# Summing the squares of a LayerNorm's variance ahead of TensorE, with one product in place of five

## The chip, the cores and the metric

The kernel runs on one core of one Trainium2 chip. The metric is the time of one execution on the device, in microseconds (us). Five engines work side by side, each on its own list of instructions and joined only by semaphores: TensorE (PE in the profile), VectorE (DVE), ScalarE (ACT), GpSimd (POOL) and SyncE (SP, which here only issues DMAs).

## The reference

One inference step of a decoder of two layers, for 512 prompt tokens and 8 sequences of 8 sample tokens, all fp32, with D = 1024 features. Cut to what matters here, a layer is

```python
def _layer_norm(x, g, b):
    mu = jnp.mean(xf, axis=-1, keepdims=True)
    var = jnp.mean(jnp.square(xf - mu), axis=-1, keepdims=True)
    return ((xf - mu) * lax.rsqrt(var + LN_EPS) * g + b)

x = _layer_norm(ALPHA * x + 0.5 * _swiglu(x, ffn1...), ln1_g, ln1_b)
h = x @ w_in          # pooling, sliding-window attention, cross-attention, gates
x = _layer_norm(ALPHA * x + merged @ w_o, ln2_g, ln2_b)
x = _layer_norm(ALPHA * x + 0.5 * _swiglu(x, ffn2...), ln3_g, ln3_b)
```

So there are three LayerNorms in each layer and six in the kernel.

## The kernel before

**Layout.** The features lie on the 128 partitions in 8 chunks (`KC`), the 576 tokens along the free axis, in two halves of 288 (`TH`). `x[:, c, half(h)]` is a tile of 128 x 288. Every weight product is split into a rounded part and a rest of the weight and of the activation, so that a step of a product is three matmuls (`mm3`); it is called a triple below.

**A LayerNorm** is done for one token half after the other: n = 0, 1, 2 is the norm of the layer, h = 0, 1 the half. A half goes round the engines in this order:

- `mean(l, n, h)`: TensorE multiplies a matrix whose entries are all 1/1024 (`ones`) with sums of the chunks and so gets the mean of every token on all partitions, in the PSUM bank `TP`. For h = 0 and for n = 1 VectorE has kept a sum of chunks (`lnsum`) and one or two products do. For h = 1 of n = 0 and n = 2 there are five products: of the sums of chunks 0+1, 2+3 and 4+5, which GpSimd adds (`add_chunks`, L1743), and of chunks 6 and 7.
- `center` (L1415): VectorE subtracts the mean, eight instructions.
- `square` (L936): ScalarE squares each centered chunk into `squares(c)`.
- `add_squares` (L1738): GpSimd adds squares 0+1, 2+3 and 4+5 (`SQUARE_SUMS`).
- `variance` (L1976, L1979): TensorE multiplies `ones` with these three sums and with squares 6 and 7, five products, into the PSUM bank `S`. An fp32 product of `ones` is two instructions in the trace.
- `root` (L940): ScalarE takes the square root; `reciprocal` (L1420): VectorE.
- `scale` (L1426) on VectorE, then ScalarE rounds the scaled chunk (`xth`, `xh`), and VectorE or GpSimd makes its rest (`rest_of_x`: L1484, L1437; GpSimd: L1754). A chunk's rounded part and rest are what TensorE needs to begin the next products with that chunk.

**Order on TensorE.** It is written out by hand, and the products of `ones` are put between the triples of whatever weight product runs then:

- n = 0 and n = 2, h = 0: mean and variance lie in `tail` of the FFN before (`tail` runs h = 0 and then h = 1, each with 8 products of 4 triples; the variance stands in the third product of h = 1). A tail's results are added onto x by VectorE, two chunks at a time (`tail_onto_x`, L1402); the four of h = 1 are placed by hand between the steps of the norm of h = 0, and the mean of h = 1 needs all four.
- n = 0, h = 1: both lie in `project_first`, which multiplies the normed x by the first columns of `w_in`: first four chunks of one block, then two blocks in turn, then two blocks into the banks S and TP, and the same again for h = 1. The mean stands after the first three chunks, the variance ahead of the two last triples of the two blocks.
- n = 1: mean and variance of h = 0 lie in the products of `w_o` (outputs m = 4 and m = 5 of h = 1), those of h = 1 in `head` of the second FFN.
- n = 2, h = 1: in layer 0 both lie in `head` of the next layer's first FFN. In layer 1 nothing comes behind: the mean and eight products of `ones` (L2330) end the kernel, and the change leaves those eight alone.

**Order on the other engines.** VectorE's list for a half is `center`, then work of the FFN or of `w_o` that is ready by then, then `reciprocal`, `scale` and the rests. That work is `tail_onto_x` (n = 0 and 2), `residual` (n = 1: the products of `w_o` onto x and into `lnsum`, L1475 and L1478), or the rest of a weight block (`rest_w`, L1164, n = 0, h = 1). GpSimd's list mixes `add_squares`, `add_chunks` and the rests of the next head's weights (L1782), in a fixed order too; in `head` of GpSimd the sums of squares stand in front of the rest of one quarter of the weights.

Of the kernel before, what the change touches and what calls it, by code (L numbers as in the profile page):

```python
# [33 lines left out]
SQUARE_SUMS = (0, 2, 4)  # L34
# [142 lines left out]
def build(nc, wblk, wg, wd, wt_d, x0, mem0, cst_d, par_d, mks_d, mvs_d, kcs_d, vcs_d, sps_d,  # L177
          y_out, kT_out, v_out, poolp_out, pools_out, mk_out, mv_out, kc_out, vc_out):
    with ExitStack() as ctx:
# [175 lines left out]
        sq_ready, sq_sum, sq_used, std_ready, normed = sem("sq_ready"), sem("sq_sum"), sem("sq_used"), sem("std_ready"), sem("normed")  # L355
# [128 lines left out]
        def square_sum_count(l, n, h, c):  # L484
            return (l * 6 + 2 * n + h) * len(SQUARE_SUMS) + SQUARE_SUMS.index(c) + 1

# [10 lines left out]
        def chunk_sum_count(fb, w):  # L497
            return fb * 3 + w + 1
# [660 lines left out]
        def _(dve):  # L1159
# [256 lines left out]

            def reciprocal(l, n, h):

                dve.wait_ge(std_ready, l * 6 + 2 * n + h + 1)
                nc.vector.reciprocal(S[:, h, 0:TH], S[:, h, 0:TH])  # L1420
                dve.drain()
# [7 lines left out]
            def norm_plain(l):  # L1429

                fb = 2 * l

                def rest_of_x(h, c):
                    if c in BY_DVE:
                        b = par[:, P_LN + 8 + c:P_LN + 9 + c]
                        dve.wait_ge(x_hi, x_hi_count(l, h, c))
                        nc.vector.scalar_tensor_tensor(out=xl[:, c, half(h)], in0=x[:, c, half(h)], scalar=b,  # L1437
                                                       in1=xh[:, c, half(h)].bitcast(F32), op0=ALU.add,
                                                       op1=ALU.subtract).then_inc(x_lo, 1)

                center(l, 0, 0)
                tail_onto_x(fb, 0, 1)
                reciprocal(l, 0, 0)
                for c in range(KC):
                    scale(0, 0, c)
                    if c > 0:
                        rest_of_x(0, c - 1)
                    if c in (1, 3, 5):
                        tail_onto_x(fb, (c + 1) // 2, 1)
                rest_of_x(0, KC - 1)  # L1450
                rest_w(pq(l, Q_IN + 1), 0)
                center(l, 0, 1)
                dve.drain().then_inc(t_free, 1)
                rest_w(pq(l, Q_IN + 1), 1)
                reciprocal(l, 0, 1)
                for c in range(KC):
                    scale(0, 1, c)
                    if c == KC - 1:
                        dve.drain().then_inc(s_free, 1)
                    if c > 0:  # L1460
                        rest_of_x(1, c - 1)
                rest_of_x(1, KC - 1)

            def norm_head(l, n):
# [32 lines left out]
                else:  # L1497
# [3 lines left out]
                for c in range(KC):  # L1501
# [5 lines left out]
                    if n == 2 and c in (1, 4):  # L1507
                        tail_onto_x(fb - 1, 1 + c // 4, 1)
                rest_of_x(0, KC - 1)
                if n == 2:  # L1510
                    tail_onto_x(fb - 1, 3, 1)
                else:
                    residual(6, 1)
                    residual(7, 1)
                center(l, n, 1)
                dve.drain().then_inc(t_free, 1)
                reciprocal(l, n, 1)
# [10 lines left out]
            def norm_last(l):  # L1528
                center(l, 2, 0)
                tail_onto_x(2 * l + 1, 0, 1)  # L1530
                reciprocal(l, 2, 0)
# [200 lines left out]
        def _(pool):  # L1732

            def add_squares(l, n, h):

                for c in SQUARE_SUMS:
                    pool.wait_ge(sq_ready, norm_count(l, n, h, c + 1))
                    nc.gpsimd.tensor_tensor(squares(c), squares(c), squares(c + 1), ALU.add).then_inc(sq_sum, 1)  # L1738

            def add_chunks(fb, w):  # L1740
# [3 lines left out]
                                        ALU.add).then_inc(chunk_sum, 1)  # L1744

# [115 lines left out]
        def _(pe):  # L1861
# [34 lines left out]
            def project_first(l, qq, u):  # L1896
# [3 lines left out]
                for h in range(2):  # L1900
                    turns = [(c, 0) for c in range(lag)] + [(c - lag * s, s) for c in range(lag, KC) for s in range(2)]
                    for c, s in turns + [(c, 1) for c in range(KC - lag, KC)]:
# [11 lines left out]
                        if (h, c, s) == (0, 6, 1):  # L1914
                            variance(l, 0, 1)
                    for s, bank in enumerate((S, TP)):
# [7 lines left out]
                        for c in range(KC):  # L1924
                            last = mm3(lambda h: bank[:, h, 0:TH], wt(s, c), (xs(xh, c), xs(xl, c)), c, KC, (h,))
                        if h == 1:
# [21 lines left out]
            def mean(l, n, h):  # L1948
# [6 lines left out]
                if n != 1 and h == 1:  # L1955

                    fb = 2 * l + n // 2
                    for w in range(3):
                        pe.wait_ge(chunk_sum, chunk_sum_count(fb, w))
                        nc.tensor.matmul(TP[:, 1, 0:TH], ones, chunk_sum_place(w), start=w == 0, stop=False)  # L1960
                    pe.wait_ge(tail_add, tail_count(fb, 3, 1))
                    for c in (KC - 2, KC - 1):
                        last = nc.tensor.matmul(TP[:, 1, 0:TH], ones, x[:, c, half(1)], start=False, stop=c == KC - 1)
                    last.then_inc(mean_done, 1)
# [6 lines left out]
            def variance(l, n, h):  # L1971
                if h == 0:
                    pe.wait_ge(s_free, s_count(l, f"var{n}") + 1)
                for c in SQUARE_SUMS:
                    pe.wait_ge(sq_sum, square_sum_count(l, n, h, c))
                    nc.tensor.matmul(S[:, h, 0:TH], ones, squares(c), start=(c == 0), stop=False)  # L1976
                for c in (KC - 2, KC - 1):
                    pe.wait_ge(sq_ready, norm_count(l, n, h, c))
                    last = nc.tensor.matmul(S[:, h, 0:TH], ones, squares(c), start=False, stop=(c == KC - 1))  # L1979
                last.then_inc(sq_used, 1)  # L1980
# [46 lines left out]
            def head(fb):  # L2027
# [26 lines left out]
                def block(g, w, h):  # L2054
                    begin_block(g, w, h)
                    for c in range(KC):
                        chunk(g, w, h, c)
                        if fb and (g, w, h, c) == ((1, 0, 0, 1) if n == 1 else (1, 0, 0, 7)):
                            variance(l, n, 1)

                for h in range(2):

                    lag = (4, 2)[h]
                    for c in range(KC + lag):
# [9 lines left out]
                        if fb and (h, c) == (0, 4 if n == 1 else KC + 1):  # L2074
# [7 lines left out]
            def tail(fb):  # L2082
# [3 lines left out]
                for h in range(2):  # L2086
                    for p in range(KC):
# [7 lines left out]
                        for i in range(4):  # L2095
# [9 lines left out]
                            if (h, p, i) == (1, 2, 1):  # L2105
# [18 lines left out]
            for l in range(L):  # L2124
# [183 lines left out]
                for h in range(2):  # L2308
                    for m in WO_HALVES[h]:
# [8 lines left out]
                        for c in range(KC):  # L2318
# [3 lines left out]
                            if (h, m, c) == (1, 5, 5):  # L2322
# [165 lines left out]
```

## Time and profile before

| | |
|---|---|
| median of 3 runs | 2364.52 us (2363.46 to 2365.7) |
| profiled execution, its own time | 2364.38 us |
| its span, first to last instruction | 2362.6 us |
| mean granted TensorE clock | 0.998 of full speed |
| busy: TensorE / VectorE / ScalarE / GpSimd | 99% / 69% / 52% / 27% |

The span is what the trace covers; 1.8 us of the execution's own time lie around it. Times in the rows below are microseconds from the span's start, unless marked ns. The engine named behind `<-` in square brackets is the one that ended an idle time.

### The profile page before, as it was taken

What the parts mean: (1) busy time and instruction counts of PE and PEld (TensorE: products, weight loads), DVE (VectorE), ACT (ScalarE), POOL (GpSimd) and SP (SyncE); (2) the same over time, 40 slices, a digit from 0 to 9 for tenths busy, and PEclk for the clock granted to TensorE, in tenths of its full rate; (3) what the DMA queues carried; (4) which work ended last, traced back from release to release, by engine and by line L of the source; (5) the groups of instructions that cost most, each with busy time, mean ns of one, the idle gap of its engine ahead of it and who ended that gap; (6) DMA issues with size and microseconds to landing.
All of it is one profiled execution on the core that took longest, in us unless ns stands there. A gap on an engine that the chain in (4) does not pass through costs nothing.

```text
span 2362.6 us, 44967 instructions
## 1 busy us (share of the span) xinstructions
PE 2329.5 (99%) x17537; PEld 2281.7 (97%) x17537; DVE 1628.8 (69%) x2722; ACT 1218.0 (52%) x2478; POOL 646.5 (27%) x573
## 2 busy tenths in 40 slices
PE   8999999999999999999999999999999999999998
PEld 8999999999999999999999999999999999999997
DVE  4878786755445787878578787766544458877775
ACT  5655555455323565555565556554552236665654
POOL 1334334230000233333423333342200021333333
PEclk9999999999999999999999999999999999999999
DMA  6222224222222122232213322333122231222221
GB/s 239 93 104 87 94 94 158 69 91 60 72 82 97 72 81 99 90 108 90 90 54 110 108 90 87 111 128 107 56 66 76 86 116 49 89 97 92 98 99 58
DMA packets 54482, 221.29 MB, mean 94 GB/s; under 512 B 15904, under 2 KB 18848, under 8 KB 41184
## 3 DMA queue, kind: packets, MB, share of 16 engines
q1 hardware_dynamic: 54272, 218.41, 27.0%
q8 instruction: 141, 2.31, 0.4%
q14 instruction: 69, 0.57, 0.1%
HBM read 213.58 MB, written 6.04 MB: 93 GB/s over the span
## 4 chain that ended last, share of the span: by engine, by line
PE 89%; DVE 7%; ACT 2%; DVEq 1%; issue 1%; DMA 0%; POOL 0%; ACTq 0%; SPq 0%; POOLq 0%
PE pair L2022 14%; PE pair L2024 14%; PE pair L2023 14%; PE pair L1865 10%; PE pair L1869 10%; PE pair L1867 10%; PE S L2022 2%; PE S L2024 2%; PE S L2023 2%; PE TP L1869 1%; PE TP L1867 1%; PE TP L1865 1%; PE TP L2203 1%; DVE htl L1260 1%; PE TP L2182 1%; PE S L1976 1%
## 5 line engine op out<-in xcount | busy, mean ns | idle before, releaser
L2023 PE MATMUL pair<-xtl,hiA 128*128 128x288 f32 x1216 | 358.8, 295 | 0.0
L2024 PE MATMUL pair<-xth,loA 128*128 128x288 f32 x1216 | 358.4, 295 | 0.0
L2022 PE MATMUL pair<-xth,hiA 128*128 128x288 f32 x1216 | 358.3, 295 | 0.0
L1766 POOL TENSOR_TENSOR loB<-rawB,hiB 128x512 fp32r<-128x512 f32 (+1 forms) x128 | 174.6, 1365 | 448.9 <-ACT hiB L719 448.9
L719 ACT ACTIVATE hiA<-TP 128x512 fp32r<-128x512 f32 (+1 forms) x372 | 194.0, 556 | 150.0 <-DVE TP L1183 72.2
L1169 DVE TENSOR_TENSOR loA<-TP,hiA 128x512 fp32r<-128x512 f32 (+1 forms) x372 | 236.3, 635 | 16.4 <-ACT hiA L719 13.2
L1766 POOL TENSOR_TENSOR loB<-rawA,hiB 128x512 fp32r<-128x512 f32 (+1 forms) x120 | 152.4, 1270 | 342.0 <-ACT hiB L719 342.0
L2024 PEld LDWEIGHTS pair<-xth,loA 128*128 128x128 f32 x1216 | 228.7, 188 | 0.0
L2023 PEld LDWEIGHTS pair<-xtl,hiA 128*128 128x128 f32 x1216 | 228.3, 188 | 0.0
L2022 PEld LDWEIGHTS pair<-xth,hiA 128*128 128x128 f32 x1216 | 228.0, 187 | 0.0
L1164 DVE TENSOR_TENSOR loA<-rawA,hiA 128x1024 fp32r<-128x1024 f32 x92 | 114.1, 1242 | 161.3 <-ACT hiA L706 160.8
L1865 PE MATMUL pair<-xh,hiA 128*128 128x288 f32 x960 | 211.5, 302 | 0.0
L1869 PE MATMUL pair<-xh,loA 128*128 128x288 f32 x960 | 205.4, 296 | 0.0
L1867 PE MATMUL pair<-xl,hiA 128*128 128x288 f32 x960 | 205.3, 295 | 0.0
L2022 PE MATMUL pair<-xth,hiB 128*128 128x288 f32 x608 | 180.6, 297 | 3.6 <-DVE c L1334 3.6
L2023 PE MATMUL pair<-xtl,hiB 128*128 128x288 f32 x608 | 179.4, 295 | 0.0
L2024 PE MATMUL pair<-xth,loB 128*128 128x288 f32 x608 | 178.8, 294 | 0.0
L2022 PE MATMUL pair<-hth,hiA 128*128 128x288 f32 x576 | 172.2, 299 | 1.6 <-DVE x L1317 1.6
L2024 PE MATMUL pair<-hth,loA 128*128 128x288 f32 x576 | 169.5, 294 | 0.0
L2023 PE MATMUL pair<-htl,hiA 128*128 128x288 f32 x576 | 169.4, 294 | 0.0
L1865 PEld LDWEIGHTS pair<-xh,hiA 128*128 128x128 f32 x960 | 153.6, 189 | 8.0 <-issue 7.0
L1782 POOL TENSOR_TENSOR wl_head<-rawA,wh_head 128x512 fp32r<-128x512 f32 x4 | 5.5, 1366 | 553.1 <-ACT wh_head L740 553.1
(400 smaller groups left out, 7012.4 us busy)
## 6 DMA issues: line engine op xcount, KB each, us to landing
rawA<-in_wblk SPq DMA_DIRECT2D x104, 512.0 KB, 3.4
rawA<-in_wg SPq DMA_DIRECT2D x44, 1024.0 KB, 4.8
rawB<-in_wg SPq DMA_DIRECT2D x44, 1024.0 KB, 4.8
rawB<-in_wd SPq DMA_DIRECT2D x24, 768.0 KB, 4.1
rawA<-in_wd SPq DMA_DIRECT2D x24, 768.0 KB, 4.4
rawA<-in_wt_d SPq DMA_DIRECT2D x4, 1024.0 KB, 4.8
rawB<-in_wt_d SPq DMA_DIRECT2D x4, 1024.0 KB, 4.9
mcs<-in_mks SPq DMA_DIRECT2D x2, 2048.0 KB, 11.3
```

The source lines that it names most:

```text
L719: nc.scalar.activation(slot((hiA, hiB), prod, n), src, ACT.Copy).then_inc(f_hi, 1)
L1164: nc.vector.tensor_tensor(lo, raw_of(qq)[0][:, s, :], hi.bitcast(F32), ALU.subtract).then_inc(w_lo, 1)
L1169: nc.vector.tensor_tensor(slot((loA, loB), prod, n), sum_bank(prod, n), slot((hiA, hiB), prod, n).bitcast(F32), ALU.subtract).then_inc(f_l ...
L1260: nc.vector.tensor_tensor(htl[:, n % 3, forms, :], hf[:, forms, :], hth[:, n % 3, forms, :].bitcast(F32), ALU.subtract).then_inc(h_lo, 1)
L1766: nc.gpsimd.tensor_tensor(slot((loA, loB), prod, n), quarter(u, prod, n), slot((hiA, hiB), prod, n).bitcast(F32), ALU.subtract).then_inc(f ...
L1865: nc.tensor.matmul(out(h), wt[0], xt[0](h), start=(kk == 0), stop=False)
L1867: nc.tensor.matmul(out(h), wt[0], xt[1](h), start=False, stop=False)
L1869: last = nc.tensor.matmul(out(h), wt[1], xt[0](h), start=False, stop=(kk == nk - 1))
L1976: nc.tensor.matmul(S[:, h, 0:TH], ones, squares(c), start=(c == 0), stop=False)
L2022: nc.tensor.matmul(bank, wt_hi, xt[0], start=start, stop=False, skip_group_check=True)
L2023: nc.tensor.matmul(bank, wt_hi, xt[1], start=False, stop=False, skip_group_check=True)
L2024: last = nc.tensor.matmul(bank, wt_lo, xt[0], start=False, stop=i == n - 1, skip_group_check=True)
```

## The change

All eight squares of a half are summed before TensorE sees them. GpSimd adds 0+1 and 2+3 and then those two sums; it no longer adds 4+5. VectorE gets a new step, `add_last_squares`: it adds 4+5, 6+7, these two sums, and GpSimd's sum of the first four, four instructions with two drains. TensorE's `variance` is then one product. This holds for all halves but the kernel's last one. In the mean of h = 1 of n = 0 and n = 2, GpSimd adds up the three pair sums as well (one more addition for each of the second and third), so that three products are left, those of chunks 6 and 7 first. Five places move in TensorE's order, and the VectorE list of n = 2 gets its `tail_onto_x` steps earlier.

```diff
-SQUARE_SUMS = (0, 2, 4)
+SQUARE_SUMS = (0, 2)
+            def add_last_squares(l, n, h):
+                for c in (4, 6):
+                    dve.wait_ge(sq_ready, norm_count(l, n, h, c + 1))
+                    nc.vector.tensor_tensor(squares(c), squares(c), squares(c + 1), ALU.add)
+                dve.drain()
+                nc.vector.tensor_tensor(squares(4), squares(4), squares(6), ALU.add)
+                dve.drain()
+                dve.wait_ge(sq_sum, first_four_count(l, n, h))
+                nc.vector.tensor_tensor(squares(4), squares(4), squares(0), ALU.add).then_inc(sq_rest, 1)
...
                 center(l, 0, 0)
                 tail_onto_x(fb, 0, 1)
+                add_last_squares(l, 0, 0)
                 reciprocal(l, 0, 0)
...
                 center(l, 0, 1)
                 dve.drain().then_inc(t_free, 1)
+                add_last_squares(l, 0, 1)
                 rest_w(pq(l, Q_IN + 1), 1)
                 reciprocal(l, 0, 1)
...
                 if n == 2:
                     tail_onto_x(fb - 1, 0, 1)
-                else:
+                add_last_squares(l, n, 0)
+                if n == 1:
                     residual(4, 1)
                     residual(5, 1)
                 reciprocal(l, n, 0)
...
-                    if n == 2 and c in (1, 4):
-                        tail_onto_x(fb - 1, 1 + c // 4, 1)
+                    if n == 2 and c in (1, 3, 5):
+                        tail_onto_x(fb - 1, (c + 1) // 2, 1)
                 rest_of_x(0, KC - 1)
-                if n == 2:
-                    tail_onto_x(fb - 1, 3, 1)
-                else:
+                if n == 1:
                     residual(6, 1)
                     residual(7, 1)
                 center(l, n, 1)
                 dve.drain().then_inc(t_free, 1)
+                add_last_squares(l, n, 1)
                 reciprocal(l, n, 1)
...
                 for c in SQUARE_SUMS:                                   # GpSimd, add_squares
...
+                pool.wait_ge(sq_sum, square_sum_count(l, n, h, 2))
+                nc.gpsimd.tensor_tensor(squares(0), squares(0), squares(2), ALU.add).then_inc(sq_sum, 1)
...
+                if w > 0:                                               # GpSimd, add_chunks
+                    pool.wait_ge(chunk_sum, chunk_sum_count(fb, w))
+                    nc.gpsimd.tensor_tensor(chunk_sum_place(w), chunk_sum_place(w), chunk_sum_place(w - 1),
+                                            ALU.add).then_inc(chunk_sum, 1)
...
-                        if (h, c, s) == (0, 6, 1):                      # project_first
-                            variance(l, 0, 1)
+                            if (h, s, c) == (0, 0, 3):                  # in its block into bank S
+                                variance(l, 0, 1)
...
-                for c in SQUARE_SUMS:                                   # variance, TensorE
-                    pe.wait_ge(sq_sum, square_sum_count(l, n, h, c))
-                    nc.tensor.matmul(S[:, h, 0:TH], ones, squares(c), start=(c == 0), stop=False)
-                for c in (KC - 2, KC - 1):
-                    pe.wait_ge(sq_ready, norm_count(l, n, h, c))
-                    last = nc.tensor.matmul(S[:, h, 0:TH], ones, squares(c), start=False, stop=(c == KC - 1))
-                last.then_inc(sq_used, 1)
+                pe.wait_ge(sq_rest, last_four_count(l, n, h))
+                nc.tensor.matmul(S[:, h, 0:TH], ones, squares(4), start=True, stop=True).then_inc(sq_used, 1)
...
-                        if fb and (g, w, h, c) == ((1, 0, 0, 1) if n == 1 else (1, 0, 0, 7)):   # head, variance
+                        if fb and (g, w, h, c) == ((1, 0, 0, 3) if n == 1 else (1, 0, 0, 7)):
-                        if fb and (h, c) == (0, 4 if n == 1 else KC + 1):                       # head, mean
+                        if fb and (h, c) == (0, 4 if n == 1 else KC - 1):
-                            if (h, p, i) == (1, 2, 1):                                          # tail
+                            if (h, p, i) == (1, 4, 2):
                                 variance(l, n, 0)
-                            if (h, m, c) == (1, 5, 5):                                          # w_o
+                            if (h, m, c) == (1, 5, 7):
                                 variance(l, 1, 0)
```

## Rows read from the trace of the kernel before

**Rows 1.** The page: busy time of each engine, its share and instructions.

```profile
PE 2329.5 (99%) x17537; PEld 2281.7 (97%) x17537; DVE 1628.8 (69%) x2722; ACT 1218.0 (52%) x2478; POOL 646.5 (27%) x573
```

**Rows 2.** Chain of waits, 429 to 443 us: start, length, what (pieces merged).

```profile
429.80 1.46 PE S L1976 x6
...
441.37 0.81 POOL xl L1754
442.22 0.40 PE pair L1865
```

**Rows 3.** Timeline of VectorE, layer 0, center and reciprocal of six halves: start, length.

```profile
407.19 3.01 DVE L1415 TENSOR_TENSOR x<-x,TP 128x288 f32<-128x288 f32 x8 [1.45 <-PE TP L1969]
413.28 1.97 DVE L1420 RECIPROCAL S<-S 128x288 f32<-128x288 f32 x1 [2.42 <-ACT S L940]
426.45 3.00 DVE L1415 TENSOR_TENSOR x<-x,TP 128x288 f32<-128x288 f32 x8
432.77 1.97 DVE L1420 RECIPROCAL S<-S 128x288 f32<-128x288 f32 x1 [1.53 <-ACT S L940]
...
777.72 3.01 DVE L1415 TENSOR_TENSOR x<-x,TP 128x288 f32<-128x288 f32 x8 [0.87 <-PE TP L1966]
785.87 1.97 DVE L1420 RECIPROCAL S<-S 128x288 f32<-128x288 f32 x1
800.52 3.01 DVE L1415 TENSOR_TENSOR x<-x,TP 128x288 f32<-128x288 f32 x8 [1.13 <-PE TP L1966]
808.23 1.97 DVE L1420 RECIPROCAL S<-S 128x288 f32<-128x288 f32 x1 [4.70 <-ACT S L940]
...
1171.51 3.01 DVE L1415 TENSOR_TENSOR x<-x,TP 128x288 f32<-128x288 f32 x8 [1.36 <-PE TP L1969]
1177.53 1.97 DVE L1420 RECIPROCAL S<-S 128x288 f32<-128x288 f32 x1 [2.35 <-ACT S L940]
1195.87 3.01 DVE L1415 TENSOR_TENSOR x<-x,TP 128x288 f32<-128x288 f32 x8 [6.36 <-PE TP L1963]
1202.78 1.97 DVE L1420 RECIPROCAL S<-S 128x288 f32<-128x288 f32 x1 [3.91 <-ACT S L940]
```

**Rows 4.** Instructions of two lines: count, duration ns min/median/max, first and last start.

```profile
L1247 DVE TENSOR_TENSOR hf<-hf x36: 457/459/460, 68.5 to 2230.0; 128x288 f32<-128x288 f32 x36
L1738 POOL TENSOR_TENSOR u<-u,u x11: 793/805/827, 410.2 to 2333.7; 128x288 f32<-128x288 f32 x11
```

**Rows 5.** Timelines of GpSimd and VectorE where both read SBUF at once.

```profile
418.29 0.81 POOL L1743 TENSOR_TENSOR hf<-x 128x288 f32<-128x288 f32 x1
418.66 0.75 DVE L1437 SCALAR_TENSOR_TENSOR xl<-x,par,xh 128x288 fp32r<-128x288 f32 x1 [0.18 <-ACT xh L975]
...
1185.94 1.04 POOL L1743 TENSOR_TENSOR c<-x 128x288 f32<-128x288 f32 x1
```

**Rows 6.** Timeline of GpSimd: weight rests behind the sums of squares, n=1 and n=2.

```profile
781.80 1.27 POOL L1782 TENSOR_TENSOR loA<-rawB,hiA 128x512 fp32r<-128x512 f32 x1 [0.36 <-ACT hiA L740]
...
1176.01 1.27 POOL L1782 TENSOR_TENSOR loB<-rawA,hiB 128x512 fp32r<-128x512 f32 x1
...
1199.95 2.51 POOL L1782 TENSOR_TENSOR loA<-rawB,hiA 128x512 fp32r<-128x512 f32 x2 [0.35 <-ACT hiA L740]
```

**Rows 7.** Timelines of VectorE and TensorE: last addition of the tail, and its successor.

```profile
421.56 0.74 DVE L1402 TENSOR_TENSOR x<-x,pair 128x576 f32<-128x576 f32 x1
422.45 1.13 PE L1960 MATMUL TP<-hf,cst 128*128 128x288 f32 x4
...
1189.56 0.40 PE L1865 MATMUL pair<-xth,hiB 128*128 128x288 f32 x1 [1.80 <-DVE x L1402]
...
2345.04 0.75 DVE L1402 TENSOR_TENSOR x<-x,pair 128x576 f32<-128x576 f32 x1 [1.37 <-PE pair L1869]
```

**Rows 8.** Busy time by stretch: length, PE, PEld, DVE, ACT, POOL, granted clock, DMA.

```profile
1205.00:1208.00 3.00, 1.47 (x10) 1.03 (x9) 2.82 (x7) 1.50 (x3) 0.00 (x0) 1.00 0.53 224
1208.00:1212.00 4.00, 3.80 (x18) 3.57 (x18) 3.86 (x10) 3.55 (x9) 0.00 (x0) 0.57 0.01 2
```

More of the change, by code:

```diff
@@ L354, in build @@
         sum_ready, chunk_sum, mean_done, cent = sem("sum_ready"), sem("chunk_sum"), sem("mean_done"), sem("cent")
-        sq_ready, sq_sum, sq_used, std_ready, normed = sem("sq_ready"), sem("sq_sum"), sem("sq_used"), sem("std_ready"), sem("normed")
+        sq_ready, sq_sum, sq_rest = sem("sq_ready"), sem("sq_sum"), sem("sq_rest")
+        sq_used, std_ready, normed = sem("sq_used"), sem("std_ready"), sem("normed")
         rot_clear, rot_in, rope_done, v_done = sem("rot_clear"), [sem("rot_in0"), sem("rot_in1")], sem("rope_done"), sem("v_done")
@@ L484, in square_sum_count, with first_four_count, last_four_count @@
         def square_sum_count(l, n, h, c):
-            return (l * 6 + 2 * n + h) * len(SQUARE_SUMS) + SQUARE_SUMS.index(c) + 1
+            return (l * 6 + 2 * n + h) * (len(SQUARE_SUMS) + 1) + SQUARE_SUMS.index(c) + 1
+        def first_four_count(l, n, h):
+            return (l * 6 + 2 * n + h + 1) * (len(SQUARE_SUMS) + 1)
+        def last_four_count(l, n, h):
+            return l * 6 + 2 * n + h + 1
         def half(h):
@@ L497, in chunk_sum_count @@
         def chunk_sum_count(fb, w):
-            return fb * 3 + w + 1
+            return fb * 5 + max(1, 2 * w)
         def chunk_in(i):
@@ L1530, in norm_last @@
                 tail_onto_x(2 * l + 1, 0, 1)
+                add_last_squares(l, 2, 0)
                 reciprocal(l, 2, 0)
@@ L1957, in mean @@
                     fb = 2 * l + n // 2
-                    for w in range(3):
-                        pe.wait_ge(chunk_sum, chunk_sum_count(fb, w))
-                        nc.tensor.matmul(TP[:, 1, 0:TH], ones, chunk_sum_place(w), start=w == 0, stop=False)
                     pe.wait_ge(tail_add, tail_count(fb, 3, 1))
                     for c in (KC - 2, KC - 1):
-                        last = nc.tensor.matmul(TP[:, 1, 0:TH], ones, x[:, c, half(1)], start=False, stop=c == KC - 1)
-                    last.then_inc(mean_done, 1)
+                        nc.tensor.matmul(TP[:, 1, 0:TH], ones, x[:, c, half(1)], start=c == KC - 2, stop=False)
+                    pe.wait_ge(chunk_sum, chunk_sum_count(fb, 2) + 1)
+                    nc.tensor.matmul(TP[:, 1, 0:TH], ones, chunk_sum_place(2), start=False, stop=True).then_inc(mean_done, 1)
                 elif n == 1:
```

## The prediction

> **What bounds the kernel now.** I read the page's busy times first: TensorE works 99% of the span [rows 1], 17,537 instructions in 2329.5 us, 0.133 us each. By that view every removed product is a gain. Then I read the chain of waits around a LayerNorm, and it says otherwise. Behind the variance of the first norm's second half [rows 2] the chain leaves TensorE: root, reciprocal, scaling, rests, and a rest by GpSimd that ends at 442.18 us, on which TensorE starts at 442.22 us. In these 10 us TensorE is busy, yet it only arrives when the loop round the other engines lets it. Such a loop runs twice in every norm: mean, center, squares, variance, reciprocal, scaling. The reader should therefore look at the VectorE timeline for the time from the end of a center to the start of its reciprocal [rows 3], not at TensorE's busy share. The order by hand hides a loop just so: the tail's last addition ends at 422.30 us and the mean that needs it is reached at 422.45 us [rows 7].
>
> **What is removed.** Six pieces of the chain are three products in 1.46 us [rows 2], so a product is 0.487 us. Eleven halves lose four products and four means lose two: 52 x 0.487 = 25.3 us of TensorE. That is the gain if TensorE bounds everywhere.
>
> **What is added.** An addition of two 128 x 288 tiles in SBUF takes VectorE 0.46 us and GpSimd 0.81 us [rows 4]. GpSimd's third addition only changes its operands; its two more chunk additions (1.6 us in each of four means) fall where GpSimd mostly waits. VectorE gets four additions for each of eleven halves, 0.46 us each with about 0.1 us for a drain: some 2 us from center's end to the finished sum (2.5 us where a `tail_onto_x` of 0.7 us comes first). This lies on the loop. Ahead, TensorE took the last squares straight from ScalarE. Behind the new waits stand VectorE's own reciprocal, at n = 1 also two residuals, at n = 0 the rest of a weight block, for which TensorE waits two blocks later. No DMA is added or moved, and GpSimd's list keeps its order. From the sum to the reciprocal I take 1.2 us: two instructions of the product at about 0.24 us, then the root (0.5 us) with its two handovers.
>
> **What the additions cost when GpSimd works too.** The GpSimd addition at 418.29 us ends at 419.10 us; VectorE's rest that began at 418.66 us ends at 419.41 us, 0.31 us behind it. In reverse, GpSimd's addition that starts at 1185.94 us while VectorE works takes 1.04 us where 0.81 is usual [rows 4, 5]. So they take turns, and a held VectorE addition ends 0.31 us after GpSimd's. The Trainium skill states it as a rule (SBUF — State Buffer, section "SBUF: two separate sides"): a VectorE instruction with two SBUF inputs and a GpSimd instruction that reads SBUF use one pair of ports under an exclusive lock, and the second waits until the first is through. By it the rival without turns, below, is out; these rows agree with it.
>
> I lay the four additions out in turns with what GpSimd has to do then: its third addition of squares, at n = 0 and 2 a chunk addition, at n = 1 one rest of weights and at n = 2 one (first half) or two (second half) [rows 6]. Each such rest is 1.27 us, comes right behind the sums, and slips in wherever VectorE drains. From center's end to the sum this makes 3.3 us (n = 0, first half), 2.6 (n = 0, second), 3.3 (n = 1, first), 2.6 (n = 1, second: GpSimd has nothing else), 4.1 and 4.6 us (n = 2). With 1.2 us behind it, center's end to reciprocal against before [rows 3]:
> - n = 0, first half: 4.5 against 413.28 - 410.20 = 3.1, so +1.4 us; second: 3.8 against 3.3, +0.5 us (the weight rest, 1.2 us, runs beside product and root).
> - n = 1, first: here 2.0 us of residuals follow the sum, 5.3 against 5.1, +0.2 us; second: 3.8 against 4.7, -0.9 us, since five products had stood late there.
> - n = 2, first: 5.3 against 3.0, +2.3 us; second: 5.8 against 3.9, +1.9 us.
>
> **Where TensorE's freed time goes.** At n = 0 the tail ends 2 us earlier for the four products, and by what the old variance waited for its squares, but the mean needs the fourth `tail_onto_x`, six scalings behind the reciprocal [rows 7]: it comes 1.4 us later, and 0.3 us more because GpSimd's additional chunk addition holds one rest. The means' two saved products vanish in that wait. The center of the second half hangs on VectorE's list, not on the mean. So the rest on which TensorE waits at 442.22 us [rows 2] comes 1.4 + 0.3 + 0.5 = **2.2 us later, in each layer**. At n = 1 the saved product time of the first half is spent waiting for the sum; TensorE reaches the second mean 0.1 us earlier, and from there the loop is 0.9 us shorter: **-1.0 us in each layer**. At n = 2 in layer 0 the fourth `tail_onto_x` moves up by three scalings and rests (2.5 us), but its reciprocal is 2.3 us later and GpSimd's additions and rests hold it: TensorE starts 0.6 us after the old 1189.56 us [rows 7]. The mean then has two products fewer (1.0 us) and two triples fewer ahead, part of which goes into waits for chunks: center 0.7 us earlier, the loop behind it 1.9 us longer, **+1.2 us**. At the end, tail addition and chunk sum come about when they did (2345.04 us [rows 7]), **0**.
>
> Sum: 2 x 2.2 - 2 x 1.0 + 1.2 = +3.6 us. To this comes the clock. From 1205 to 1208 us TensorE was busy for half of the time, at full clock; in the 4 us behind, with work at hand, its mean granted clock was 0.57, most of it at the 1.2 GHz level [rows 8], which loses 4 x 0.43 = 1.7 us. The change makes TensorE idle longer ahead of means and variances; I take one more such stretch on the path, 1.7 us. **+5.3 us**: on the profiled execution's 2364.38 us (span 2362.6 and 1.8 around it, 0.1 us below the median) that is **2369.7 us**.
>
> **Rivals.**
> - *TensorE bounds after all*: 25.3 us less, 2339 us. For it: 99% busy. Against it: the chain of rows 2.
> - *The additions don't take turns*, or GpSimd is through before (**the other side**). Then the sum is ready 2.1 us (2.5 behind a tail addition) after center: n = 0 +0.6 us a layer (3.7 against 3.1, 3.3 against 3.3), n = 1 -2.2 us (4.1 against 5.1, 3.5 against 4.7), n = 2 -3.0 us (the earlier `tail_onto_x` and the shorter mean count in full, less 0.7 us of additions). 1.2 - 4.4 - 3.0 = -6.2: 2358.2 us. It decides from the point where VectorE's four additions take under 2.2 us. Against it: rows 5.
> - *They take turns, but the weight rests fall outside*, for a quarter's DMA or rounding comes later, and the clock holds: n = 0 +2.0, n = 1 -1.8, n = 2 -1.0: -0.6, 2363.8 us. The change does little, then.
> - *The clock falls in many places*: ahead of the n = 0 means (one in each layer), at n = 2 and at the kernel's end, where TensorE would be idle for 3 us just ahead of the mean and eight products. Four such stretches of 1.7 us on top of 3.6, 10.4 us in all: about 2375 us. Against it: 2 us of idle time up to 1189.56 us left the next matmuls fast [rows 7].
>
> **How the numbers follow.** Forecast 0.45 (own range 2367 to 2373), without rests 0.22, many clock falls 0.20, no turns 0.10, TensorE 0.03. About 0.2%, 4.7 us, is what a measurement of this kernel tells from no change. The forecast lies 0.6 us over that line, so I split it, 0.25 slower and 0.20 the same. Slower 0.25 + 0.20 = 0.45, the same 0.20 + 0.22 = 0.42, faster 0.13. The range takes in the cases at both ends but the 25 us one, 2358 to 2376 us.
>
> **What would show it.** In the profile of the changed kernel: VectorE's additions of squares with 0.46 us where GpSimd rests and 0.8 us or more where it works; center to reciprocal at about 4.5, 3.8, 5.3, 3.8, 5.3, 5.8 us; new TensorE waits on VectorE's fourth `tail_onto_x` ahead of the mean at n = 0 (2 us or more) and on the sum at the variances; TensorE's busy share near 98%. I am wrong if center to reciprocal stays at or below its old length at n = 0 and n = 2, or if TensorE passes the mean of the second half at n = 0 without a wait.

## The result, and the profile after

The changed kernel takes 2371.13 us (median of 10 runs, 2370.48 to 2372.98) against 2364.87 us before (10 runs, 2363.46 to 2365.7): 6.3 us longer, a ratio of 1.0028 with a 95% interval of 1.0020 to 1.0036. The forecast was 2369.7 us, 5.3 us over the profiled execution before. The profiled execution of the changed kernel took 2370.7 us, with a span of 2368.9 us.

The page's busy times answer [rows 1]:

```profile
PE 2310.2 (98%) x17433; PEld 2265.7 (96%) x17433; DVE 1660.3 (70%) x2766; ACT 1217.4 (51%) x2478; POOL 655.2 (28%) x581
```

TensorE has 104 instructions less and is busy for 19.3 us less, and yet the kernel is longer: what was removed is now waiting time. VectorE has the 44 new additions and 31.5 us more. Shared out among them that is 0.72 us for each, where 0.46 us was the time of an addition alone [rows 4].

The VectorE timeline of layer 0 answers [rows 3]. The columns are start, length, line, operation, tiles and, in brackets, the idle time ahead and its end. L1422 is the center, L1428 (twice), L1430 and L1433 are the four additions of `add_last_squares`, L1438 the reciprocal. The two halves of n = 0 and the second of n = 2 stand in full, of the others center and reciprocal:

```profile
406.07 3.01 DVE L1422 TENSOR_TENSOR x<-x,TP 128x288 f32<-128x288 f32 x8 [1.45 <-PE TP L1994]
...
409.66 0.64 DVE L1428 TENSOR_TENSOR u<-u,u 128x288 f32<-128x288 f32 x1
410.23 1.06 DVE L1428 TENSOR_TENSOR c<-c,c 128x288 f32<-128x288 f32 x1
411.37 0.46 DVE L1430 TENSOR_TENSOR u<-u,c 128x288 f32<-128x288 f32 x1
411.90 0.46 DVE L1433 TENSOR_TENSOR u<-u,hf 128x288 f32<-128x288 f32 x1
413.77 1.97 DVE L1438 RECIPROCAL S<-S 128x288 f32<-128x288 f32 x1 [1.42 <-ACT S L947]
...
428.04 3.00 DVE L1422 TENSOR_TENSOR x<-x,TP 128x288 f32<-128x288 f32 x8
431.17 1.01 DVE L1428 TENSOR_TENSOR u<-u,u 128x288 f32<-128x288 f32 x1
432.11 0.45 DVE L1428 TENSOR_TENSOR c<-c,c 128x288 f32<-128x288 f32 x1
432.63 0.46 DVE L1430 TENSOR_TENSOR u<-u,c 128x288 f32<-128x288 f32 x1
433.16 0.46 DVE L1433 TENSOR_TENSOR u<-u,hf 128x288 f32<-128x288 f32 x1
...
434.97 1.97 DVE L1438 RECIPROCAL S<-S 128x288 f32<-128x288 f32 x1 [0.22 <-ACT S L947]
...
779.46 3.01 DVE L1422 TENSOR_TENSOR x<-x,TP 128x288 f32<-128x288 f32 x8 [0.87 <-PE TP L1991]
...
787.54 1.96 DVE L1438 RECIPROCAL S<-S 128x288 f32<-128x288 f32 x1
...
802.29 3.00 DVE L1422 TENSOR_TENSOR x<-x,TP 128x288 f32<-128x288 f32 x8 [0.89 <-PE TP L1991]
...
809.25 1.97 DVE L1438 RECIPROCAL S<-S 128x288 f32<-128x288 f32 x1 [1.35 <-ACT S L947]
...
1172.59 3.01 DVE L1422 TENSOR_TENSOR x<-x,TP 128x288 f32<-128x288 f32 x8 [1.36 <-PE TP L1994]
...
1181.13 1.97 DVE L1438 RECIPROCAL S<-S 128x288 f32<-128x288 f32 x1 [1.42 <-ACT S L947]
...
1196.79 3.01 DVE L1422 TENSOR_TENSOR x<-x,TP 128x288 f32<-128x288 f32 x8 [2.86 <-PE TP L1989]
1199.93 1.02 DVE L1428 TENSOR_TENSOR u<-u,u 128x288 f32<-128x288 f32 x1
1200.87 0.45 DVE L1428 TENSOR_TENSOR c<-c,c 128x288 f32<-128x288 f32 x1
1201.39 1.37 DVE L1430 TENSOR_TENSOR u<-u,c 128x288 f32<-128x288 f32 x1
1202.84 1.36 DVE L1433 TENSOR_TENSOR u<-u,hf 128x288 f32<-128x288 f32 x1
...
1205.55 1.97 DVE L1438 RECIPROCAL S<-S 128x288 f32<-128x288 f32 x1 [1.35 <-ACT S L947]
```

Read it as the prediction read [rows 3], start plus length of the center to start of the reciprocal, in us:

| half | before | forecast | after | center's end to sum: forecast, after |
|---|---|---|---|---|
| n = 0, first | 3.1 | 4.5 | 4.69 | 3.3, 3.28 |
| n = 0, second | 3.3 | 3.8 | 3.93 | 2.6, 2.58 |
| n = 1, first | 5.1 | 5.3 | 5.07 | 3.3, 3.33 |
| n = 1, second | 4.7 | 3.8 | 3.96 | 2.6, 2.61 |
| n = 2, first | 3.0 | 5.3 | 5.53 | 4.1, 4.12 |
| n = 2, second | 3.9 | 5.8 | 5.75 | 4.6, 4.40 |

Why four equal additions take from 0.45 to 1.38 us is seen on GpSimd's timeline: the third addition of squares at n = 0 (L1761) and the chunk addition behind it (L1766), and the two weight rests of n = 2, second half (L1809):

```profile
409.18 0.81 POOL L1761 TENSOR_TENSOR hf<-hf 128x288 f32<-128x288 f32 x1
409.95 1.02 POOL L1766 TENSOR_TENSOR hf<-x 128x288 f32<-128x288 f32 x1
...
1200.87 3.02 POOL L1809 TENSOR_TENSOR loA<-rawB,hiA 128x512 fp32r<-128x512 f32 x2 [0.23 <-ACT hiA L747]
```

GpSimd's addition ends at 409.99 us, VectorE's first at 410.30; the chunk addition ends at 410.97, VectorE's second at 411.29: 0.31 and 0.32 us behind, as in [rows 5]. Of the 44 additions 20 are held so, each to 0.31 or 0.32 us behind a GpSimd instruction's end. It works the other way too: the two rests take 3.02 us where two took 2.51 [rows 6].

**Where the time went.** The start of a center marks where a kernel stands in its work. Shifts against the kernel before, each counted from the first center (whose start, ahead of all changed work, lies between 406.07 and 407.55 us in the twelve traces, earliest in that of the changed kernel), give what each stage of each kernel costs. A stage runs from the first center of its norm to the first of the next, the last one to the kernel's last center. In us:

| kernel | median, and against before beside it | n = 0 | n = 1 | n = 2 | n = 0 | n = 1 | end | sum |
|---|---|---|---|---|---|---|---|---|
| forecast | +5.3, with 1.7 for the clock | +2.2 | -1.0 | +1.2 | +2.2 | -1.0 | 0 | +3.6 |
| the change | 2371.13, +6.3 | +2.86 | -0.66 | +1.34 | +3.48 | -0.31 | +0.72 | +7.4 |
| e1, means only | 2362.08, -2.0 | +0.25 | +0.11 | -2.40 | -0.16 | +0.16 | +0.12 | -1.9 |
| e2, variances only | 2375.51, +11.5 | +3.65 | -0.64 | +4.71 | +2.82 | -0.27 | +2.04 | +12.3 |
| e3, variances at n = 1 only | 2362.41, -1.6 | +0.23 | -0.80 | +0.03 | -0.92 | -0.36 | -0.06 | -1.9 |
| e4, weight rests wait | 2368.05, +4.0 | +2.74 | -0.49 | -0.76 | +3.46 | -0.24 | +0.06 | +4.8 |
| e5, GpSimd sums no squares | 2367.75, +3.8 | +2.79 | -1.63 | -0.41 | +1.84 | -1.28 | +2.10 | +3.4 |
| e6, tail's wait filled | 2369.84, +5.9 | +2.49 | -0.80 | +1.29 | +1.87 | -0.40 | +0.71 | +5.2 |
| e7, old places | 2383.82, +19.9 | +5.49 | +1.63 | +2.56 | +5.39 | +1.71 | +3.23 | +20.0 |
| e8, means and n = 1 | 2359.98, -4.0 | -0.29 | -0.73 | -2.47 | -0.18 | -0.32 | +0.13 | -3.9 |
| e9, old places filled | 2373.32, +9.2 | +1.33 | +0.02 | +1.53 | +2.55 | +1.81 | +1.64 | +8.9 |
| e10, one place moved | 2360.05, -4.1 | +0.05 | -0.78 | -3.14 | +0.01 | -0.33 | +0.12 | -4.1 |

The first n = 0 column and the next two are layer 0, the others layer 1. Kernels without any edit at a stage differ there by some 0.3 us, once by 0.9 (e3, second n = 0); smaller differences are not read. For the change the sum is 7.4 us and the execution 6.3 us longer, since its first center was 1.1 us early, ahead of anything that the change touches.

**The piece that wasn't forecast.** The chain of waits of the changed kernel from the first variance to the fourth `tail_onto_x` at n = 0 (start, length, what):

```profile
412.50 0.74 PE S L2000 x2
...
416.94 0.52 DVE xl L1455
417.46 0.68 DVE x L1409
418.18 0.61 PE pair L1892
418.79 0.24 PE pair L1894
419.03 0.24 PE pair L1896
...
421.90 0.13 PE pair L1892
...
423.13 0.75 DVE x L1409
```

Behind the variance TensorE has fifteen matmuls, then waits for the second `tail_onto_x` (L1409), and then its matmuls follow each other at 0.24 us where 0.13 is usual, for 3.4 us; the fourth `tail_onto_x`, at 423.13 us, waits for them. The stretch tells it as a clock. The views of busy time by stretch, 417 to 421 us, of the kernel before, the changed one and e6 (length, PE, PEld, DVE, ACT, POOL, granted clock, DMA):

```profile
417.00:421.00 4.00, 4.00 (x33) 4.00 (x32) 3.75 (x7) 2.41 (x6) 2.84 (x4) 1.00 0.00 0
```

```profile
417.00:421.00 4.00, 2.82 (x12) 2.82 (x13) 3.82 (x8) 2.37 (x5) 2.91 (x4) 0.63 0.00 0
```

```profile
417.00:421.00 4.00, 2.97 (x20) 2.46 (x19) 3.64 (x8) 3.00 (x6) 2.23 (x3) 1.00 0.00 0
```

After 3.0 us without work TensorE did part of the tail at 1.2 GHz. In e6 that idle time is filled. Between the first norm and the last center the kernel before has one stretch of low clock, the one of [rows 8]. The changed kernel has three: this one, its counterpart in layer 1 (granted clock 0.50 from 1582 to 1585.4 us) and one at n = 2 (0.50 from 1186 to 1189.4 us). The old one is gone there: from 1205 to 1213 us the clock is 1.00.

### The profile page after: what moved, and what is told of

It reads as the page before. It is cut to its first block, busy times and chain, and to the rows that moved or that the text cites. A ratio compares the mean times of both kernels' runs of the same rounds, so it can differ in the third digit from the quotient of the medians.

```text
span 2368.9 us, 44833 instructions
## 1 busy us (share of the span) xinstructions
PE 2310.2 (98%) x17433; PEld 2265.7 (96%) x17433; DVE 1660.3 (70%) x2766; ACT 1217.4 (51%) x2478; POOL 655.2 (28%) x581
## 4 chain that ended last, share of the span: by engine, by line
PE 84%; DVE 9%; ACT 4%; DVEq 1%; issue 1%; DMA 0%; ACTq 0%; POOL 0%; SPq 0%
PE pair L2042 14%; PE pair L2044 14%; PE pair L2043 13%; PE pair L1892 9%; PE pair L1896 9%; PE pair L1894 9%; PE S L2042 2%; PE S L2044 2%; PE S L2043 2%; PE TP L1896 1%; PE TP L1892 1%; PE TP L1894 1%; PE TP L2223 1%; DVE htl L1267 1%; DVE S L1438 1%
## 5 line engine op out<-in xcount | busy, mean ns | idle before, releaser
L1809 POOL TENSOR_TENSOR wl_head<-rawA,wh_head 128x512 fp32r<-128x512 f32 x4 | 5.6, 1400 | 551.4 <-ACT wh_head L747 551.3
```

## The experiments

**Means against variances.** The first question was which part of the change costs. e1 keeps the change's means and sets the variances back, e2 does the reverse:

```diff
 e1:                 # asked in add_last_squares, add_squares and variance; the places as before too
+        def summed(l, n, h):
+            return False                # five products as before
 e2:                 # GpSimd, add_chunks
-                if w > 0: ... add chunk_sum_place(w - 1)
                     # mean: five products; tail_onto_x and the mean's place as before
```

> The change's means alone (three products, GpSimd's two chunk additions more in each, the fourth tail_onto_x at n = 2 moved up), with the five products of each variance, their additions and their places as before. Theory (the additions of squares on VectorE cost the time): n = 0 loses 0.3 us in each layer, n = 2 gains 1 to 2 us (tail_onto_x three scalings earlier, two products fewer), in sum -1 us, about 2364 us. Rival (the longer time comes from GpSimd's added chunk additions, on which the mean now waits): +3 us or more, 2368 us.

Measured: 2362.08 us, 2.0 us less than before (ratio 0.9990, interval 0.9982 to 0.9999). The gain lies at n = 2 alone, -2.40 us. It stands at the second center already, at 1193.6 us, which comes 2.8 us earlier counted from the first; so it isn't the clock, which in e1 holds where the kernel before has the slow stretch of [rows 8], from 1208 us on. At n = 0 the second center comes 0.30 us late in both layers, the price that the prediction gave GpSimd's added addition there, and the second half's center to reciprocal is 3.00 us in place of 3.32, which makes it good. The rival is out.

> The change's variances alone (one product, seven additions, new places), with means and the order of tail_onto_x as before. Theory (additions in turns, n = 0 +1.9 us in each layer, n = 1 -1.0, n = 2 +2 to +3, clock +1.7): +6 to +8 us, 2371 to 2373 us, no better than the whole change. Rival (the means bring the loss): at most +3 us, 2368 us.

Measured: 2375.51 us, +11.5 us (1.0049, 1.0035 to 1.0063). The variances bring the loss, and more of it than the +6 to +8 us that I expected. Most of the miss is n = 2, +4.71 us instead of 2 to 3, and the end, +2.04 us. At both places TensorE's clock fell where it held in the change. In e2 TensorE waits 3.53 us for the second half's sum at n = 2 and its granted clock from 1209 to 1213 us is 0.57; at the end it waits 2.27 us for the second `tail_onto_x` and the clock from 2352 to 2356 us is 0.58. In the change the clock is 1.00 from 1205 to 1213 us and from 2340 to 2356 us.

The means' gain within the whole change is thus 4 to 5 us, more than the 2.0 us that they bring alone. Up to the second center of n = 2, counted from the first, it is the same: 2.8 us earlier in e1 than before, 2.7 us earlier in the change than in e2. Behind it e1 gives 0.8 us back (center to reciprocal 4.70 us in place of 3.90), while e2 loses a further 0.6 us (6.34 us against the change's 5.75) and 1.3 us more than the change at the end. What the low clocks of e2 have in this was not tested by itself.

**n = 1 alone.**

```diff
+        def summed(l, n, h):
+            return n == 1        # one product there, five elsewhere; means as before
```

> One-product variances at n = 1 alone (four of the eleven), everything else as before. Theory (at n = 1 VectorE has its residuals behind the sum anyway, and the second half's loop is 0.7 us shorter): -0.7 us in each layer, -1.4 us, about 2363.5 us. Rival (each added VectorE addition costs, wherever it stands): +2 us, 2367 us. Rival (products removed are a gain of their 0.487 us, sixteen of them): -7.8 us, 2357 us.

Measured: 2362.41 us, -1.6 us (0.9994, 0.9985 to 1.0003, so not told from no change by the runs alone). In the stages of n = 1 it is -0.80 and -0.36 us. In its trace the second half's center to reciprocal is 3.96 us, the first's 5.10. Sixteen products fewer are not worth their 7.8 us, and added additions don't cost wherever they stand.

**The turns.** Two runs take the two engines apart. In e4 GpSimd stays away with its weight rests until VectorE's sum is done:

```diff
                 nc.gpsimd.tensor_tensor(squares(0), squares(0), squares(2), ALU.add).then_inc(sq_sum, 1)
+                if n > 0:
+                    pool.wait_ge(sq_rest, last_four_count(l, n, h))
```

> The whole change, and at n = 1 and n = 2 GpSimd waits for VectorE's finished sum before it takes its next work (weight rests), so that these don't take turns with VectorE's additions. Theory (turns): at n = 2 center's end to reciprocal falls from 5.5 and 5.75 us to 4.6 and 3.9 us, at n = 1 the first half's sum comes 0.9 us earlier; rests come 1.5 to 2.5 us later, which costs less: 2368 to 2370 us. Rival (the additions cost by their number, not by turns): the intervals stay, the rests are late, 2371 us or more.

Measured: 2368.05 us, 3.1 us below the change's median and +4.0 us against before where the change has +6.3. VectorE at n = 2, second half:

```profile
1201.66 0.45 DVE L1428 TENSOR_TENSOR c<-c,c 128x288 f32<-128x288 f32 x1
1202.18 0.46 DVE L1430 TENSOR_TENSOR u<-u,c 128x288 f32<-128x288 f32 x1
1202.71 0.46 DVE L1433 TENSOR_TENSOR u<-u,hf 128x288 f32<-128x288 f32 x1
1204.53 1.97 DVE L1438 RECIPROCAL S<-S 128x288 f32<-128x288 f32 x1 [1.35 <-ACT S L947]
```

The same two additions took 1.37 and 1.36 us in the changed kernel. Center's end to reciprocal is 4.02 and 3.94 us at n = 2 (4.6 and 3.9 expected), and that stage goes from +1.34 to -0.76 us. At n = 1, first half, the sum is 0.9 us earlier as expected, but the reciprocal is not (5.96 us in place of 5.07): the residuals stand between, and the rests now fall on them (their two additions into `lnsum` take 1.21 and 1.49 us in place of 0.46). The turns are real, and moving the partner moves the cost: here it paid at n = 2, where VectorE has nothing else to do behind the sum, and not at n = 1.

In e5 GpSimd leaves its three additions out, and VectorE's wait for them goes with them:

```diff
             def add_squares(l, n, h):          # GpSimd
-                for c in SQUARE_SUMS: ... squares(c) + squares(c + 1), then squares(0) + squares(2)
+                pass
```

> The whole change, but GpSimd's three additions of squares are left out (three of the eight squares are missing in the variance; VectorE still makes its four additions). Theory (turns): where GpSimd has nothing else then (second halves at n = 0 and n = 1) center's end to reciprocal falls from 3.94 to 3.4 us, as four undisturbed additions of 0.46 us give it; at the other halves GpSimd's chunk addition or weight rest still takes its turn, some 0.5 us less there; time 3 to 4 us less than the whole change, 2367 to 2368 us. Rival (VectorE's additions cost by their number alone): intervals and time stay, 2371 us.

Measured: 2367.75 us, as expected in sum, but not place by place. VectorE at n = 0, second half:

```profile
431.20 0.46 DVE L1428 TENSOR_TENSOR u<-u,u 128x288 f32<-128x288 f32 x1
431.58 0.46 DVE L1428 TENSOR_TENSOR c<-c,c 128x288 f32<-128x288 f32 x1
432.11 0.46 DVE L1430 TENSOR_TENSOR u<-u,c 128x288 f32<-128x288 f32 x1
432.64 0.46 DVE L1432 TENSOR_TENSOR u<-u,hf 128x288 f32<-128x288 f32 x1
434.46 1.97 DVE L1437 RECIPROCAL S<-S 128x288 f32<-128x288 f32 x1 [0.22 <-ACT S L947]
```

3.39 us from center's end to reciprocal in place of 3.93. But the first half of n = 0 comes only to 4.49 us from 4.69 (0.5 us less was expected; the chunk addition takes the free turn), against 3.08 us before. So of the 1.6 us that this half lost, 0.2 us went with GpSimd's additions of squares; the four additions and the wait behind them keep the rest. And n = 0 still costs 2.79 and 1.84 us: without GpSimd's squares the change would still be slower than before. Most of the gain came at n = 1 and at n = 2, where the second half went from 5.75 to 4.31 us (0.5 us less was expected): one of its additions is held there in place of three. The end costs more than in the change (+2.10 against +0.72 us), with a granted clock of 0.57 from 2343 to 2347 us.

**The clock.** In e6 TensorE gets products that nobody reads where it would wait:

```diff
+                        if (h, p) == (1, 6):                  # tail, ahead of the second tail_onto_x
+                            for _ in range(4):
+                                nc.tensor.matmul(S[:, 1, 0:TH], ones, lnsum[:, half(1)], start=True, stop=True)
```

> The whole change, and four products with ones, whose result nothing reads, in the tail where TensorE waits 2.2 to 3.0 us for the second tail_onto_x (four places, 7.8 us of TensorE work in all). Theory (the idle time ahead of it lets the clock fall, and at n = 0 the slow triples hold the fourth tail_onto_x by 0.75 us): granted clock from 0.63 to 1.00 in the stretch behind, second center at n = 0 some 0.75 us earlier in each layer, 1.5 to 2.5 us less than the whole change, 2369 us. Rival (the clock is off the path there): 2371 us. Rival (TensorE's work counts): 2371 + 7.8 = 2379 us.

Measured: 2369.84 us, 1.3 us below the change's median; against the runs of before beside each it is +5.9 and +6.3 us, so the medians alone leave 0.4 to 1.3 us. The trace is clearer: the granted clock from 417 to 421 us is 1.00 (row above), and the first matmuls behind the wait follow each other at 0.13 us after the first:

```profile
418.86 0.40 PE L1892 MATMUL pair<-hth,hiB 128*128 128x288 f32 x1 [1.03 <-DVE x L1409]
419.10 0.29 PE L1894 MATMUL pair<-htl,hiB 128*128 128x288 f32 x1
419.22 0.29 PE L1896 MATMUL pair<-hth,loB 128*128 128x288 f32 x1
```

The second center at n = 0 is late by 1.90 us in both layers, against 2.71 and 2.75 us in the changed kernel: 0.8 us for the clock in each layer, as expected. At n = 2 and at the end nothing changed (+1.29 and +0.71 against +1.34 and +0.72). At n = 2 the change's TensorE waits 2.93 us and then has a granted clock of 0.50 from 1186 to 1189.4 us, in e6 it is 1.00; but there VectorE's scalings, rests and tail additions come last, and the second center comes only 0.15 us earlier. Behind it e6 has a stretch of low clock again, 0.58 from 1205 to 1209 us, as the kernel before had [rows 8], and this costs nothing that shows. At the end the change's wait of 2.24 us left the clock at 1.00, so that there was nothing to gain. TensorE had 16 products more (7.8 us at 0.487 us each), and the kernel got no longer.

**The places.** e7 is the whole change with each variance where it stood before in TensorE's order:

```diff
-                            if (h, p, i) == (1, 4, 2):      # tail; and likewise the other three places
+                            if (h, p, i) == (1, 2, 1):
```

> The whole change, with each variance at its old place in TensorE's order (up to nine triples earlier). Theory (the loop of the other engines sets when the sum is ready): TensorE waits for the same sums, at n = 0 for 3 to 4 us in place of 0.6, and does the triples behind it instead of waiting for tail_onto_x: time within 1.5 us of the whole change, 2370 to 2372.5 us. Rival (the new places carry the loss): 2366 us or less. Rival (the new places save it from worse): 2375 us or more.

Measured: 2383.82 us, +19.9 us (1.0085, 1.0071 to 1.0098), 12.7 us over the whole change (13.6 us by the runs of before beside each). My expectation was wrong: I had taken the order of waiting and working as free. Busy time by stretch around the first variance, e7 and then e9:

```profile
409.00:413.50 4.50, 0.38 (x3) 0.24 (x2) 3.99 (x8) 1.39 (x4) 2.68 (x4) 0.78 0.50 198
413.50:418.00 4.50, 4.50 (x18) 4.21 (x19) 2.78 (x3) 0.73 (x2) 0.00 (x0) 0.50 0.00 0
```

```profile
409.00:413.50 4.50, 3.87 (x18) 2.79 (x17) 3.42 (x6) 0.90 (x4) 2.11 (x3) 1.00 0.37 152
413.50:418.00 4.50, 4.50 (x37) 4.50 (x36) 3.81 (x5) 1.80 (x4) 0.00 (x0) 1.00 0.00 0
```

In e7 TensorE waits for the sum in one piece, doing 3 instructions in 4.5 us, and then works for 4.5 us at a granted clock of 0.50 (18 instructions, where 37 go at full clock). The triples behind are those that the tail additions wait for, so it is paid on the path. e9 is e7 with unread products in these waits:

```diff
+                if n != 1:                                       # variance, ahead of its wait
+                    for _ in range(7 if h == 0 else 5 if n == 0 else 4):
+                        nc.tensor.matmul(S[:, 1, 0:TH], ones, lnsum[:, half(1)], start=True, stop=True)
```

> The run with the old places again (2383.8 us), and in the waits ahead of the variances at n = 0 and n = 2 (4.4, 3.4, 5.2 and 3.0 us) 7, 5, 7 and 4 products whose result nothing reads. Theory (one long wait ahead of a block of triples lets the clock fall, and TensorE then sets the end of the tail): granted clock from 0.50 to 1.00 in the 4.5 us behind the first variance, n = 0, n = 2 and the end get back most of 2.7 + 2.5 + 1.2 + 2.4 us, n = 1 keeps its 3.7 us: 2375 to 2377 us. Rival (the triples behind the variance, which come later, hold the tail at any clock): 2381 us or more.

Measured: 2373.32 us, 10.5 us below e7, more than I expected. By stages 9.6 of 11.1 us come back at n = 0, n = 2 and the end, where the waits were filled. So the clock was most of the loss at the old places. The new places of the change split the wait at n = 0, 0.6 us at the variance and 3.0 us later; that all they are worth lies in this is argued and not shown.

The other 1.5 us come back at n = 1, where nothing was filled. TensorE waits there for the first half's sum, 2.52 us in layer 0 and 2.51 us in layer 1. Busy time by stretch behind these two waits in e9:

```profile
785.00:789.00 4.00, 4.00 (x31) 3.95 (x30) 3.13 (x4) 2.15 (x4) 2.08 (x2) 1.00 0.00 0
1948.00:1952.00 4.00, 3.90 (x17) 3.64 (x18) 1.81 (x5) 1.59 (x4) 0.41 (x1) 0.60 0.00 2
```

After the same wait the clock held in layer 0 and fell in layer 1, and the stages cost +0.02 and +1.81 us. In e7 it fell behind both waits (0.57 from 790 to 794 us, 0.59 from 1957 to 1961 us), and they cost +1.63 and +1.71 us. Why it held once stays open. At full clock the old places of n = 1 cost 0.7 us more than the new ones (+0.02 against -0.66).

**A better version.** e8 joins e1 and e3:

```diff
+        def summed(l, n, h):
+            return n == 1        # with the change's means
```

> The change's means and its one-product variances at n = 1, with the variances at n = 0 and n = 2 as before. Theory: the two gains lie in different stages and add up, -2.0 and -1.6 us: about 2360.5 us. Rival (the gain of one is given back by the other's wait): 2362 us.

Measured: 2359.98 us, -4.0 us against before (0.9983, 0.9974 to 0.9992), and 10 to 11 us less than the change: the gains add up. In its trace one wait stood out at n = 2, second half: VectorE waits 4.71 us for the root although the squares are there. e10 moves that variance:

```diff
-                        if fb and (g, w, h, c) == ((1, 0, 0, 3) if n == 1 else (1, 0, 0, 7)):
+                        if fb and (g, w, h, c) == ((1, 0, 0, 3) if n == 1 else (1, 0, 0, 5)):
```

> Means and one-product variances at n = 1 alone (2360.0 us), and the five-product variance of the second half at n = 2 two triples earlier in TensorE's order. There the squares are summed at 1195.5 us and TensorE comes at 1196.2 us. Theory: VectorE's wait for the root, 4.7 us from center's end, becomes 0.7 us shorter, 2359.3 us. Rival (TensorE waits for GpSimd's third sum, and loses what VectorE gains): 2360 us.

Reciprocal of that half in e8, then in e10:

```profile
1199.34 1.97 DVE L1445 RECIPROCAL S<-S 128x288 f32<-128x288 f32 x1 [4.71 <-ACT S L953]
```

```profile
1198.69 1.97 DVE L1445 RECIPROCAL S<-S 128x288 f32<-128x288 f32 x1 [3.90 <-ACT S L953]
```

Measured: 2360.05 us, -4.1 us (0.9983, 0.9974 to 0.9992). The wait is 0.81 us shorter, and the stage goes from -2.47 to -3.14 us, but the time of the whole kernel can't be told from e8's. Whether the 0.7 us are real gain or lost behind stays open.

## Why the prediction was right

**The mechanism held.** That a loop round the other engines sets the time at the norms, and not TensorE's list, was the first step; the change took 52 products away (25.3 us by the prediction's rows, 19.3 us of busy time on the page) and lost 6 us, e6 added 16 products and lost nothing. The rival of a bound TensorE is out.

**The turns held, to 0.2 us.** The six sums came 2.58 to 4.40 us behind their centers, forecast 2.6 to 4.6. The Trainium skill (SBUF — State Buffer, section "SBUF: two separate sides") says that VectorE's instruction with two SBUF inputs and a GpSimd instruction that reads SBUF lock each other out for the whole instruction; the 20 held additions, each ending 0.31 or 0.32 us behind GpSimd's, agree, and so does e4, where the partner was moved and 1.37 us became 0.46. (0.31 us is less than the 0.46 us of an addition alone, so these rows don't show that all of a held addition waits.) The rival without turns is out, and so is the one with the weight rests outside: at n = 2, second half, two rests hold two additions to 1.37 and 1.36 us. What was undersized is the piece behind the sum: 1.35 to 1.42 us to the reciprocal at five of the six halves and not 1.2. That is 0.1 to 0.2 us in each half, and explains why n = 0 came to 4.69 and 3.93 us, and why the second half of n = 1 gained 0.74 and not 0.9 us.

**The stages.** n = 2 was right as a sum (+1.34 against +1.2), not in its terms: the second center came 0.16 us earlier and not 0.7, the loop behind it was 1.85 us longer as forecast (1.9), and 0.36 us came back behind the reciprocal. n = 1 gave -0.66 and -0.31 where -1.0 was forecast; in e3, alone, -0.80 and -0.36. At n = 0 the working gave +1.7 us to the second center, and with the clock held (e6) it is 1.90 us. Its second half was right too, 3.93 - 3.32 = 0.6 us against 0.5. The end gave +0.72 us where nothing was forecast; its first half lost 1.6 us between center and reciprocal as at n = 0, and the tail did not take all of that up. By stages the change costs 7.4 us where 5.3 were forecast, and the 6.3 us of the whole contain a first center that came 1.1 us early. So that the total came within 1.0 us of the forecast is in part luck.

**The clock: the size right, the place wrong.** The step "I take one more such stretch on the path, 1.7 us" measured 2 x 0.8 = 1.6 us, at n = 0 in each layer. That one stretch of 1.7 us and two of 0.8 us make about the same is luck. The low clock at n = 2 costs nothing that shows, and at the end the clock doesn't fall ahead of the last center. The place is the one that the rival of many clock falls named. The step that failed is the one that ruled it out there, "2 us of idle time ... left the next matmuls fast". That was true for the row it quotes (1.80 us of idle time), but the change makes it 3.0 us. And the wait is not where the text put it. It said that TensorE would wait for the fourth `tail_onto_x` and that passing the mean without a wait would show it wrong. TensorE passed the mean without a wait, since it waited earlier, for the second tail addition, whose bank the seventh product of the tail needs, and then came late itself. By that sign the step was wrong, though the time agrees.

**What the prediction did not price.** The new places of the variances have no term of their own in the sum. e7 shows that they carry 12.7 us: without them the change would have cost 20 us. And the two parts of the change were never priced one by one. They have opposite signs, -2.0 and +11.5 us alone, and within the second part n = 1 gains.

## What to carry to other kernels

Price what is taken from a nearly fully busy engine by the loop that feeds it: look at the time from the event that starts the loop to the one that ends it, and count every instruction put into it, with the partner that it takes turns with. Where a wait on TensorE grows past what its neighbours show, ask at which clock the work behind it will run; moving the waiting product was worth 12.7 us here, filling the waits with unread products 10.5 us in one kernel and 0.8 us at each of two places in another. And undo a change part by part before judging it: two of its parts together made a kernel 4 us faster than before.

## What was unexpected of the hardware

- Work that nobody reads made a kernel faster: e9, which fills e7's waits at n = 0 and n = 2, takes 10.5 us less, 9.6 of 11.1 us by stages where it fills them. Behind the first variance the granted clock was 1.00 and not 0.50.
- 3.0 us without work in the change and 4.1 us in e7 were followed by the 1.2 GHz level (granted clock 0.63 from 417 to 421 us and 0.50 from 413.5 to 418 us); with the wait cut to 1.03 us in e6 it was not. In between, the length of the wait alone did not decide: 2.24 us (the change, at the end) and 2.52 us (e9, n = 1, layer 0) left the full clock, 2.27 us (e2, at the end) and 2.51 us (e9, n = 1, layer 1) were followed by the low one.
- Taking turns costs both sides: two weight rests took 3.02 us with VectorE's additions between and 2.51 us without.
